# A decoder layer with product-key experts: split value products from the middle of the seventh streamed half to the end, on three buffer sets

## The reference, cut to what matters

```python
def block(args):
    xt, it, gt = args                                   # 128 tokens of one block
    act = gelu(einsum('td,ted->te', xt, u_tab[it]))     # dots with the picked rows of u
    return einsum('te,ted->td', gt * act, v_tab[it])    # sum of the picked rows of v
```

## Time and profile before

| what | value |
|---|---|
| median of 3 runs | 4100.17 us (4097.18 to 4105.68) |
| profiled execution, its own time | 4106.96 us |
| its span | 4105.1 us |
| PE, DVE, ACT, POOL busy | 90%, 66%, 30%, 39% |
| granted TensorE clock, mean | 0.953 |
| DMA | 276 GB/s over the span |

### The profile page before, as it was taken

One profiled execution on the slowest core, in us unless ns is written; L12 is line 12 of the kernel. 1 busy time (PEld: TensorE's weight loads), 2 busy tenths in 40 slices (PEclk: granted clock), 3 DMA queues, 4 the chain that ended last, 5 costly groups with the idle time before them and its releaser, 6 DMA issues.

```text
span 4105.1 us, 46071 instructions
## 1 busy us (share of the span) xinstructions
PE 3706.4 (90%) x14431; PEld 2467.1 (60%) x14431; DVE 2709.5 (66%) x5504; ACT 1238.0 (30%) x2640; POOL 1580.5 (39%) x1341
## 2 busy tenths in 40 slices
PE   6999989898888979867769899798999999999998
PEld 5778768677777768656434454453544545445763
DVE  1445542348778866666999989889876868743540
ACT  1333332232333232225342240330422404224530
POOL 2556534331222147655344443443454444410000
PEclk8999999899999989988889999899999999999999
DMA  7666633347766658878899999999999999963557
GB/s 237 203 223 218 211 103 93 97 157 238 233 220 222 219 177 262 275 237 313 315 362 391 361 391 368 353 388 356 381 402 393 406 404 394 398 266 125 185 199 275
DMA packets 506183, 1133.96 MB, mean 276 GB/s; under 512 B 41036, under 2 KB 250364, under 8 KB 505760
## 3 DMA queue, kind: packets, MB, share of 16 engines
q1 hardware_dynamic: 334976, 570.93, 40.2%
q0 software_dynamic: 147456, 536.94, 35.0%
q10 hardware_dynamic: 23584, 24.12, 1.7%
HBM read 1044.80 MB, written 89.41 MB: 276 GB/s over the span
## 4 chain that ended last, share of the span: by engine, by line
PE 34%; DVE 14%; DMA 3%; issue 2%; ACT 1%; POOL 0%; DVEq 0%; ACTq 0%; SPq 0%
PE ps L1390 27%; DVE u_ring L2399 6%; PE ps L1376 4%; PE ps L1422 2%; DMA u_ring<-in_peer_u,pidx 1%; DMA v_ring<-in_peer_v 1%; DVE split_v L2446 1%; ACT split_v L1846 1%; DVE hot L2391 1%; DVE hot L2392 1%; DVE pick_own L2002 0%; DVE pick_own L1997 0%; DVE got_own L2005 0%; PE h_up L1365 0%; DVE inds_own L1960 0%
## 5 line engine op out<-in xcount | busy, mean ns | idle before, releaser
L1390 PE MATMUL ps<-v_ring,table 128*128 128x512 f32 x3584 | 1593.1, 596 | 16.6 <-DMA v_ring<-in_peer_v 16.6
L993 POOL DMA_INDIRECT u_ring<-in_peer_u,pidx x800 | 772.1, 965 | 969.8 <-DVE coefe L2399 902.0
L1390 PEld LDWEIGHTS ps<-v_ring,table 128*128 128x128 f32 x3584 | 664.1, 191 | 772.2 <-issue 723.7
L2399 DVE CUSTOM_DVE_ANT_0 u_ring<-u_ring,h_up 128x1024 f32<-128x1024 f32 x800 | 948.1, 1218 | 140.4 <-DMA u_ring<-in_peer_u,pidx 125.1
L1052 PE MATMUL ps<-x_hi,w_hi 128*128 128x512 f32 x1280 | 516.1, 403 | 39.7 <-ACT w_hi L1498 23.6
L1055 PE MATMUL ps<-x_lo,w_hi 128*128 128x512 f32 x1280 | 506.0, 395 | 0.0
L937 POOL TENSOR_TENSOR w_lo<-w_raw,w_hi 128x1024 fp32r<-128x1024 f32 x120 | 302.1, 2522 | 196.5 <-ACT w_hi L1498 190.7
L1376 PEld LDWEIGHTS ps<-hot,hot 128*128 128x128 f32 x2048 | 282.0, 203 | 155.2 <-issue 112.6
L1814 ACT ACTIVATE table<-ps 128x512 f32<-128x512 f32 (+3 forms) x256 | 229.5, 896 | 438.4 <-PE ps L1376 391.7
L958 POOL DMA_INDIRECT e_ring<-in_peer_u,icole x224 | 233.7, 1043 | 290.4 <-DVE dotse L2057 210.9
L1802 ACT ACTIVATE hot<-hot,by_slot 128x128 f32<-128x128 f32 x1024 | 322.3, 389 | 73.4 <-DVE hot L2391 51.6
(11 more groups left out here) (332 smaller groups left out, 4266.5 us busy)
## 6 DMA issues: line engine op xcount, KB each, us to landing
v_ring<-in_peer_v SPq DMA_DIRECT2D x576, 512.0 KB
w_raw<-in_w_in SPq DMA_DIRECT2D x88, 512.0 KB
wh_d<-w_hi SPq DMA_DIRECT2D x56, 512.0 KB, 2.7
wl_d<-w_lo SPq DMA_DIRECT2D x56, 512.0 KB, 4.2
w_hi<-wh_d SPq DMA_DIRECT2D x56, 512.0 KB
w_lo<-wl_d SPq DMA_DIRECT2D x56, 512.0 KB
u_ring<-in_peer_u,pidx POOLq DMA_INDIRECT x800
raw_mid<-in_w_branch SPq DMA_DIRECT2D x48, 256.0 KB
```

The lines of the kernel that those rows point to most:

```text
L993: pool.indirect_dma_start(out=u_ring[:, slot_of(n, k), :], out_offset=None, in_=u_tab, in_offset=bass.IndirectOffsetOnAxis(ap=pidx[n % 2][ ...
L1390: last = pe.matmul(ps[2 * (n % 2) + c][:, :], table[:, row_of(n, i1), :], v_ring[:, j % V_TILES, HALF * c:HALF * c + HALF], start=(n == p ...
L2399: dve.tensor_tensor_reduce(out=u_ring[:, slot_of(n, k), :], in0=u_ring[:, slot_of(n, k), :], in1=h1_up[:, :, :].rearrange("p c n -> p (c n)"),
```

## The change

The split products now start at tile 32 of the seventh half and go on through the eighth and the ninth (`FIRST_SPLIT`). There are three sets of buffers (SPLITS) in place of two: six rows of `u_ring` for the values, and for the coefficients two places in `score_in` and the seventh row of `u_ring`, since the one-hot tiles are still in use in the seventh half. The high parts of the coefficients move from ACT to DVE, as one copy for both blocks (`c_made`), except in the ninth half, where ACT makes them (`c_last`). The low parts of the coefficients become one subtraction for both blocks (`rows_at` takes the two table rows with a stride). The value slots of all split tiles come free at the low part.

```diff
@@ -67,6 +67,7 @@
 DOT_TILES = HALF_T - 4
 TURN_TILE = HALF_T - 2
 EARLY_DOTS = 72
+SPLITS = 3
 SEARCH_TILES = 6
 PICK_TILE = HALF_T // 2
 
@@ -433,8 +434,10 @@
         raw_pq = [raw_at(f"raw_pq{b}", r_top + 4 * NB * D + 4096 * b, KD) for b in range(2)]
         assert r_top + 4 * NB * D + 8192 <= where["m_hi"]
         split_v = [[nc.alloc_sbuf_tensor_at(f"split_v{part}_{i}", [P, D], F32R, offset=where["u_ring"] + (2 * i + part) * D * 4)
-                    for part in range(2)] for i in range(2)]
-        split_c = [nc.alloc_sbuf_tensor_at(f"split_c{i}", [P, 2, 2, P], F32R, offset=where[f"hot1_{i}"]) for i in range(2)]
+                    for part in range(2)] for i in range(SPLITS)]
+        split_c = [nc.alloc_sbuf_tensor_at(f"split_c{i}", [P, 2, 2, P], F32R, offset=o)
+                   for i, o in enumerate((where["score_in"], where["score_in"] + 2 * D, where["u_ring"] + 2 * SPLITS * D * 4))]
+        assert 2 * SPLITS < U_ROWS
 
         def late_topk_tiles(free):
 
@@ -542,7 +545,7 @@
         hot_one, hot_ready, hot_scaled = sem("hot_one"), sem("hot_ready"), sem("hot_scaled")
         turned, paired, build_out = sem("turned"), sem("paired"), sem("build_out")
         closed, summed = sem("closed"), sem("summed")
-        high_made, low_made, split_used = sem("high_made"), sem("low_made"), sem("split_used")
+        c_made, c_last, high_made, low_made, split_used = sem("c_made"), sem("c_last"), sem("high_made"), sem("low_made"), sem("split_used")
         FA = Steps(sem("fin_act"), ["sq"], seed=0)
         FV = Steps(sem("fin_dve"), "st ag ep mg rc sb".split(), seed=0)
         p_out = sem("p_out")
@@ -609,9 +612,22 @@
         def in_flight(p):
             return range(max(p - 1, 0), min(p, NBLK - 1) + 1)
 
-        def last_split(p, i):
-
-            return NTILE * (p - NBLK + 1) + i
+        FIRST_SPLIT = NTILE * (NBLK - 2) + HALF_T
+
+        def split_at(p, i):
+
+            return NTILE * p + i - FIRST_SPLIT
+
+        def rows_at(p, i):
+
+            rows = sorted(row_of(n, tile_key(p, i)) for n in in_flight(p))
+            return table[:, rows[0]:rows[-1] + 1:max(rows[-1] - rows[0], 1), :]
+
+        def high_rows(p, i):
+            return (c_last, i + 1) if p == NBLK else (c_made, split_at(p, i) + 1)
+
+        def part_of(n, p, i):
+            return sorted(in_flight(p), key=lambda m: row_of(m, tile_key(p, i))).index(n)
 
         def tile_key(p, i):
 
@@ -883,11 +899,11 @@
 
                 j = NTILE * p + i
                 first = P * tile_key(p, i)
-                old = j - V_TILES - NTILE * (NBLK - 1)
-                if old in range(NTILE):
+                old = j - V_TILES - FIRST_SPLIT
+                if old >= 0:
                     sp.wait_ge(low_made, old + 1)
                 else:
-                    sp.wait_ge(v_used, j + 1 - (NTILE if old >= NTILE else 0))
+                    sp.wait_ge(v_used, j + 1)
                 sp.dma_start(v_ring[:, j % V_TILES, :], v_tab[first:first + P, :]).then_inc(v_in[j % V_TILES], 16)
 
             sp.wait_ge(e_out, 32)
@@ -1406,25 +1422,27 @@
 
             def split_values_of(p, i):
 
-                m = last_split(p, i)
-                vhi, vlo = split_v[m % 2]
-                c_of = split_c[m % 2]
+                m = split_at(p, i)
+                vhi, vlo = split_v[m % SPLITS]
+                c_of = split_c[m % SPLITS]
                 for n in in_flight(p):
                     if n == p and i == 0:
                         pe.wait_ge(summed, p - 1)
                     for a, v in ((0, vhi), (0, vlo), (1, vhi)):
                         if n == in_flight(p)[0]:
                             if a == 0 and v is vhi:
+                                pe.wait_ge(*high_rows(p, i))
                                 pe.wait_ge(high_made, m + 1)
                             elif a == 0:
                                 pe.wait_ge(low_made, m + 1)
                         for c in range(2):
-                            last = pe.matmul(ps[2 * (n % 2) + c][:, :], c_of[:, n % 2, a, :], v[:, HALF * c:HALF * c + HALF],
+                            last = pe.matmul(ps[2 * (n % 2) + c][:, :], c_of[:, part_of(n, p, i), a, :], v[:, HALF * c:HALF * c + HALF],
                                              start=(n == p and i == 0 and a == 0 and v is vhi),
                                              stop=(n == p - 1 and i == NTILE - 1 and a == 1))
                     if n == p - 1 and i == NTILE - 1:
                         last.then_inc(closed, 1)
-                last.then_inc(split_used, 1)
+                if p < NBLK or i < NTILE - 1:
+                    last.then_inc(split_used, 1)
 
             turn(0)
             raise_h1(1)
@@ -1445,7 +1463,7 @@
                             raise_h1(p + 2)
                     if i >= HALF_T and p + 1 < NBLK:
                         pair(p + 1, i - HALF_T)
-                    if p != NBLK - 1:
+                    if split_at(p, i) < 0:
                         values_of(p, i)
                     else:
                         split_values_of(p, i)
@@ -1834,16 +1852,15 @@
 
             def high_parts(p, i):
 
-                j, m = NTILE * p + i, last_split(p, i)
+                j, m = NTILE * p + i, split_at(p, i)
                 act.wait_ge(v_in[j % V_TILES], 16 * (j // V_TILES) + 16)
                 if m == 0:
                     act.wait_ge(u_dots, dots_before(NBLK, 0) + U_ROWS)
-                    act.wait_ge(build_out, pair_item(NBLK - 1, NSUB - 1) + 1)
-                if m >= 2:
-                    act.wait_ge(split_used, m - 1)
-                for n in in_flight(p):
-                    act.activation(split_c[m % 2][:, n % 2, 0, :], table[:, row_of(n, tile_key(p, i)), :], ACT.Copy)
-                act.activation(split_v[m % 2][0][:, :], v_ring[:, j % V_TILES, :], ACT.Copy).then_inc(high_made, 1)
+                if m >= SPLITS:
+                    act.wait_ge(split_used, m - SPLITS + 1)
+                if p == NBLK:
+                    act.activation(split_c[m % SPLITS][:, 0:1, 0, :], rows_at(p, i), ACT.Copy).then_inc(c_last, 1)
+                act.activation(split_v[m % SPLITS][0][:, :], v_ring[:, j % V_TILES, :], ACT.Copy).then_inc(high_made, 1)
 
             turn_out(0)
             for sub in range(NSUB):
@@ -1857,7 +1874,7 @@
                         pair_out(p, NSUB - 1)
                     if i == 4 and p >= 2:
                         root(p - 2)
-                    if p == NBLK - 1:
+                    if split_at(p, i) >= 0:
                         high_parts(p, i)
                     if p < NB:
                         part = topk_at(p, i)
@@ -2437,14 +2454,19 @@
 
             def low_parts(p, i):
 
-                j, m = NTILE * p + i, last_split(p, i)
+                j, m = NTILE * p + i, split_at(p, i)
+                c_of = split_c[m % SPLITS][:, 0:len(in_flight(p)), :, :]
+                vhi, vlo = split_v[m % SPLITS]
+                if p == NBLK - 1 and i == 0:
+                    dve.wait_ge(build_out, pair_item(NBLK - 1, NSUB - 1) + 1)
+                if p < NBLK:
+                    if m >= SPLITS:
+                        dve.wait_ge(split_used, m - SPLITS + 1)
+                    dve.tensor_copy(c_of[:, :, 0, :], rows_at(p, i)).then_inc(c_made, 1)
                 dve.wait_ge(high_made, m + 1)
-                vhi, vlo = split_v[m % 2]
-                for n in in_flight(p):
-                    dve.tensor_tensor(out=split_c[m % 2][:, n % 2, 1, :], in0=table[:, row_of(n, tile_key(p, i)), :],
-                                      in1=split_c[m % 2][:, n % 2, 0, :].bitcast(F32), op=ALU.subtract)
-                last = dve.tensor_tensor(out=vlo[:, :], in0=v_ring[:, j % V_TILES, :], in1=vhi[:, :].bitcast(F32), op=ALU.subtract)
-                last.then_inc(low_made, 1)
+                dve.wait_ge(*high_rows(p, i))
+                dve.tensor_tensor(out=c_of[:, :, 1, :], in0=rows_at(p, i), in1=c_of[:, :, 0, :].bitcast(F32), op=ALU.subtract)
+                dve.tensor_tensor(out=vlo[:, :], in0=v_ring[:, j % V_TILES, :], in1=vhi[:, :].bitcast(F32), op=ALU.subtract).then_inc(low_made, 1)
 
             split_keys(0)
             for sub in range(NSUB):
```

## The result

The changed kernel takes 4077.13 us in the median of 5 runs (4073.42 to 4082.83), the kernel before 4105.68 over the 5 runs made beside it (4097.18 to 4106.86): ratio 0.9936, with a 95% interval of 0.9922 to 0.9951. It is faster, by some 26 us (20 to 32), not by 39.

The account below looks back on a forecast made before the run. PE was taken to bound the kernel, with waits for DVE's low part in B and value-tile supply binding C after the change. Gains 24 + 15 + 0 = 39 us from 4100.2 gave 4061, range 4046 to 4075.

Parts of the forecast that it names:

- stage A: Second half of the seventh streamed half, 32 tiles: split products cut a tile from 4.33 to 3.58 us, 24 us gained.
- Stage B: Eighth half, 64 tiles, already split: a third buffer set removes PE's wait for DVE's low part, 15 us gained.
- the chain: ACT's copies, then DVE's subtractions, until a tile's low part is made: 3.1 us in Stage B, 2.85 in Stage C.
- Stage C: Ninth half, 64 tiles, plain to split products: supply of value tiles binds, so 0 gained, 114 us as before.
- round: One cycle of the four value slots in Stage C, landing plus chain: 7.15 us, 1.79 a tile.
- the landing: Time from a value load's issue until its data is there: 4.3 us taken in Stage C, bounds 3.0 and 5.6.
- the ring: Four value-tile slots, each held from load issue until the low part frees it; claimed to bind Stage C at 1.79 us a tile.
- rival 2: In Stage C, bursts of three loads and DVE's steps make the round 7.7 to 7.9 us: total 4069, chance 0.10.
- Rival 1: Loads in Stage C land as they do alone, round 5.85 to 6.25 us: total 4045 to 4050, chance 0.20.
- Rival 3: Stage A doesn't speed up because ACT or DVE, with three handshakes a tile, need 4.3 us: total 4085, chance 0.05.
- Rival 4: PE idle a quarter of each tile in Stage C lowers the granted clock to 1.2 GHz: total 4119, chance 0.04.
- Rival 5: The change doesn't act, as another wait takes over in Stage A and Stage B: 4100, chance 0.02.

## Why the prediction was right or wrong

**Wrong: the size.** 4061 was forecast with a range of 4046 to 4075, 4077 was measured. The difference is 16 us. Of it, 5.5 is the point that it set out from: the prediction took 4100.2, and the kernel before measured again gave 4105.7; the range had no room for that drift, though A's start moves by 15 us between traces. The other 10.5 are in the sum, 39 against some 26 to 28: stage A gave 1 to 2 us less, B 1 to 2 less, and C lost 9 where nothing was forecast.

**Stage A: right, 24 against 22.6.** A tile was to take 3.58 us and takes 3.63. DVE was to need 3.2 and ACT 3.1 a tile; they were busy 2.9 and 3.0 (92.4/32 and 97.2/32) beside PE, which has no gap. The copy of 128x256, in no row before, took 0.28 us, inside its bounds of 0.2 to 0.45.

**Stage B: right in size, 15 against 13.3, half right in reason.** The step said that the third set takes the wait away. It does (175.3 us by itself), but the moved copy does so nearly as well (176.8 by itself): without ACT's two coefficient copies ahead of the value copy the chain is short enough for two sets. The prediction counted the copy's move as a relief of ACT's load and did not put it into the chain of the earlier trace rows. A tile takes 2.72 in place of 2.69.

**Stage C: the step that failed.** "C gains nothing: 0" stood on a round of 4.3 us of landing and 2.85 of chain, 7.15 in all. The mechanism was right: the ring binds, not PE, ACT or DVE, and more slots take C to DVE's bound. The term that was mis-sized is the landing. It was set to 4.3, below the 4.5 that the earlier trace rows showed, because the crowd would be thinner; it was 4.6 in the median and 4.95 in the mean of tiles 14 to 59, and in a sum of rounds it is the mean that counts. The chain was 2.75, even below the 2.85. So the round is 7.7. The crowd is thinner only in the mean, 1.93 us from load to load: a slot comes free when DVE is done with it, and after a wait several tiles follow each other at DVE's own pace, so a third of the loads are issued 1.3 to 1.4 us apart. That these bursts are what keeps the landing long fits, but no run shows it by itself.

The prediction laid C out as 27 us until the low part of tile 15, twelve rounds, and 1 us for the last products. In the trace these are 29.7, 92.3 (twelve rounds of 7.69) and 1.2. The rounds account for 6.5 of the 9 us, the slower beginning for 2.7, of which 1 lies within what C differs between traces (28.6 us to tile 15 where A is plain). The prediction had the right value for the case: "by 5.0 as a mean 122 (8 lost)". It is also rival 2, given 0.10: "Loads in bursts of three and DVE's steps make the round 7.7 to 7.9: C 122". C took 123.2.

**The other rivals.** Rival 1, loads landing as when alone, is out: in C the landing never fell below 4.3 in the median, even with three slots. In stage A of the changed kernel, with 3.6 us between tiles and for most loads no other under way, it was 3.5:

```profile
v_ring<-in_peer_v SPq DMA_DIRECT2D x32, 512.0 KB, 3.5
```

So that is what a lone load costs here; the 3.0 of the earlier trace rows ends at the last data, not at the signal. The Trainium skill, page DMA: Bandwidth & Descriptors, section Anatomy of one DMA, fits 2.0 us plus bytes over 436 GB/s, for a DMA issued from GpSimd, which makes 3.2 us of 512 KB. The trace comes near it in A (3.5) and disagrees with it in C by 1.4 us (4.6). Rival 3 is out by A's 3.63 us a tile. Rival 4, the clock: C's granted clock stayed at 1.00 with PE busy 102 of 123 us. Rival 5 is out by all stages.

What stays open is why a load lands 0.8 us later among others than in A when the DMA engines are busy only 0.71 of the time (three slots). The runs show the size, not the cause.

## What to carry to other kernels

Where a ring feeds a stage, the time per tile is at least (issue to landing + landing to free slot)/slots. A change that makes the consumer faster but holds the slot longer, as a copy and a subtraction in place of one product, can lose. Before a faster form goes into a stage, work out the round with the mean landing that the trace shows in a crowd, and not with less in the hope of a thinner one, and give the ring more slots first, from buffers that are dead by then. Where a wait goes away after several edits, try each alone: here either of two was enough in B, and in C, where only the third set applies, that set is worth 10 us.

## What the runs showed of the hardware that was not expected

The time from issue to landing of a 512 KB load grew while the DMA still had room, as the 324 GB/s with seven slots show. In the changed kernel the median was 3.5 us in A (155 GB/s), 4.2 in B (200) and 4.6 in C (262); in C it was 4.3 with three slots (220) and, for the loads into the added buffers, 5.0 with five (299) and 6.0 with seven (324). The number of loads under way and the data rate rise together in all of these, so no run tells which of the two does it.

```profile
v_ring<-in_peer_v SPq DMA_DIRECT2D x64, 512.0 KB, 4.2
```

```profile
v_more<-in_peer_v SPq DMA_DIRECT2D x11, 512.0 KB, 5.0
```

```profile
v_more<-in_peer_v SPq DMA_DIRECT2D x24, 512.0 KB, 6.0
```

(the view of DMA issues: in B of the changed kernel, then in C with five slots and with seven). A copy of 128x256 float32 to fp32r on DVE takes 0.28 us, less than the subtraction of the same shape, 0.43:

```profile
3652.49 0.28 DVE L2465 CAST split_c<-table 128x256 fp32r<-128x256 f32 x1
...
3653.28 0.43 DVE L2468 TENSOR_TENSOR split_c<-table,split_c 128x256 fp32r<-128x256 f32 x1 [0.51 <-ACT split_v L1863]
```
